# One product with the state for new values and outputs, outputs kept by token rows, and moved loads, in a DeltaNet and attention encoder layer

## What is computed

```python
proj = rms_norm(h) @ w_in                # q, k, v of the delta rule, z, a, b, attention q, k, v, two gates
# delta rule, both directions, 8 value heads on 4 key heads, chunks of 64 tokens
v_new = u_i - w_i @ state
o     = qd_i @ state + aqk_i @ v_new
state = state * exp(gl_i) + kd_i.T @ v_new
o_dn  = rms_norm(o_fwd + o_bwd, dn_out_norm) * silu(z)      # norm over the 128 numbers of a head
y_dn, y_at = o_dn @ w_dn_branch, attention(q, k, v) @ w_attn_branch
h = h + (sigmoid(gate_dn) * y_dn + sigmoid(gate_at) * y_at) @ w_o
h = h + square(relu(rms_norm(h) @ w_up)) @ w_down           # then a gated per-layer embedding
```

## Time and profile before

| What | us |
|---|---|
| median of 3 runs (lowest to highest) | 3044.26 (3043.36 to 3045.45) |
| profiled execution | 3044.7 |
| its span in the trace | 3042.9 |
| PE busy in the span | 2870.0 (94%) |
| DVE, ACT, POOL busy | 1537.4, 915.6, 318.0 |

### The profile page before, as it was taken

The page is one execution under the profiler, slowest core; times in us unless marked ns, Lnnn a source line. Parts: engine busy times, 40 slices in busy tenths (PEclk is TensorE's granted clock), DMA queues, the critical chain, the costliest instruction groups (busy, mean ns, idle before and its releaser), DMA issues. The chain is left out here.

```text
span 3042.9 us, 40696 instructions
## 1 busy us (share of the span) xinstructions
PE 2870.0 (94%) x17223; PEld 2430.7 (80%) x17223; DVE 1537.4 (51%) x2164; ACT 915.6 (30%) x1238; POOL 318.0 (10%) x418
## 2 busy tenths in 40 slices
PE   6999989997996999799999999999999999999999
PEld 5878878886785999688886788888888888888787
DVE  4556638995782443477753423333433433433732
ACT  4674432123440222244434502321111112112321
POOL 0000110000004666100002100100000000000200
PEclk8999999998997999899999999999999999999999
DMA  6227874226347565311125541111111111110121
GB/s 196 64 88 181 233 226 128 78 82 190 119 128 199 169 183 147 125 36 36 35 76 195 205 145 61 35 42 35 40 37 35 42 35 35 42 35 28 57 63 50
DMA packets 304516, 299.65 MB, mean 98 GB/s; under 512 B 53494, under 2 KB 258880, under 8 KB 303568
## 3 DMA queue, kind: packets, MB, share of 16 engines
q1 hardware_dynamic: 297840, 261.47, 28.9%
q0 software_dynamic: 6496, 35.59, 3.5%
HBM read 205.67 MB, written 84.79 MB: 95 GB/s over the span
## 5 line engine op out<-in xcount | busy, mean ns | idle before, releaser
L176 ACT ACTIVATE w_hi<-w_stage 128x1024 fp32r<-128x1024 f32 x149 | 157.2, 1056 | 930.4 <-PE psum L1637 928.7
L1637 PE MATMUL psum<-x_hi,w_hi 128*128 128x512 f32 (+1 forms) x1536 | 386.3, 360 | 7.6 <-issue 4.7
L1637 PE MATMUL psum<-x_lo,w_hi 128*128 128x512 f32 (+1 forms) x1536 | 383.7, 358 | 0.0
L1637 PE MATMUL psum<-x_hi,w_lo 128*128 128x512 f32 (+1 forms) x1536 | 383.2, 358 | 0.0
L701 PE MATMUL psum<-u_hi,w_hi 128*128 128x512 f32 (+1 forms) x1272 | 344.7, 380 | 7.5 <-PEq L218 7.5
L1920 DVE TENSOR_TENSOR tail_h<-tail_h,psum 128x1280 f32<-128x1280 f32 x136 | 202.1, 1486 | 248.9 <-PE psum L1637 248.9
L701 PE MATMUL psum<-u_lo,w_hi 128*128 128x512 f32 (+1 forms) x1272 | 321.1, 361 | 0.0
L701 PE MATMUL psum<-u_hi,w_lo 128*128 128x512 f32 (+1 forms) x1272 | 319.8, 360 | 0.0
L1637 PEld LDWEIGHTS psum<-x_hi,w_hi 128*128 128x128 f32 x1536 | 256.2, 188 | 53.9 <-issue 7.8
L1637 PEld LDWEIGHTS psum<-x_lo,w_hi 128*128 128x128 f32 x1536 | 255.6, 188 | 45.5
L1637 PEld LDWEIGHTS psum<-x_hi,w_lo 128*128 128x128 f32 x1536 | 255.5, 188 | 45.5
(11 more groups left out here) (217 smaller groups left out, 3943.6 us busy)
## 6 DMA issues: line engine op xcount, KB each, us to landing
w_stage<-in_w_in_dram SPq DMA_DIRECT2D x53, 512.0 KB, 4.9
w_stage<-in_w_up_dram SPq DMA_DIRECT2D x32, 512.0 KB, 4.2
w_stage<-in_w_down_dram SPq DMA_DIRECT2D x32, 512.0 KB, 3.7
dc_rows<-rows_gc_beta SPq DMA_DIRECT2D x40, 256.0 KB, 6.2
gates<-pj_out SPq DMA_DIRECT2D x16, 640.0 KB, 2.9
st_v<-dn_v SPq DMA_DIRECT2D x20, 512.0 KB, 6.3
st_decay<-rows_decay SPq DMA_DIRECT2D x20, 512.0 KB, 6.7
dn_o<-st_ob SPq DMA_DIRECT2D x80, 128.0 KB, 2.0
```

The costliest lines, as they stand in the source:

```text
L176: e.activation(self.hi[:, J % 2, :] if out is None else out, src, ACT.Copy).then_inc(self.high_done, 1)
L1637: ins = e.matmul(acc_chunk(core, t % 2, c), wt[:, k, cols], x(k)[:, n0:n1], start=(k == 0 and n == 0), stop=(k == n_k - 1 and n == 2))
```

## The change

Five parts.

1. The order of the projection tiles: the ropes stand at 20, 22, 24, 36, 38 and so on to 48, each with a plain tile behind it, and a plain slot of the solves has room for 13600 instead of 13000 modelled nanoseconds, a rope slot 5800 instead of 5200.
2. The first iteration's inputs of the delta phase are loaded inside `phase_proj`, on SP at its last weight-load step, ahead of the store of the last tile, into a set of buffers `first`, which lies over buffers of the ropes. The four inverse loads wait for POOL's stores of the inverses (`u_stored`). The attention's first queries, keys and values are loaded by SP inside `phase_delta`, behind the third iteration's inputs.
3. In a unit, the `w` rows and the scaled queries lie in one ring (`nq`, half of `w`, `qd`, other half of `w`), so that one 128-column stationary block times the state gives new values in one half of the partitions and outputs in the other. `from_state` is gone. The product of `aqk` is turned round (`aqk` 64 x 64 stationary, new values moving), so outputs come by token rows. PE's order in a turn of the loop is new_values(n, 0), new_values(n-1, 1), w_rows(n+1), from_values(n, 0), from_values(n-1, 1). Copies that took 128 partitions in one go take 64 in two.
4. `dn_o` is laid out by tokens ([2, TOK, VH*P]); a unit stores four DMAs of 64 rows of 1 KB instead of two of 256 rows of 512 B. The tail loads a head as 1280 rows of 512 B for each direction.
5. The head norm in the tail goes by token rows: DVE sums squares over a row (`tensor_reduce`), ACT takes a small square root, DVE a reciprocal and a broadcast multiply, PE turns the head back with ten transposes inside the next column tile (`turn_head`), and DVE applies gain and z straight from PSUM (`gate_head`). The three ones matmuls, the Ln, the Exp and their table loads, and the two DVE multiplies go. POOL no longer waits for its store to land before it loads the next head.

The core of the diff:

```diff
 def proj_tiles():
-    order += [("z", 0), ("rope", 0), ("rope", 1), ("rope", 2)]
-    late_rope = (38, 39, 40, 41, 44, 46, 48)
+    ropes_at = (20, 22, 24, 36, 38, 40, 42, 44, 46, 48)
...
 def solve_shares():
-            room += 5200 if ... == "rope" else 13000
+            room += 5800 if ... == "rope" else 13600
...
 # phase_proj, SP
+                    if t == N_IN - 1:
+                        heads_are_stored(e)
+                        load_state_inputs(e, 0, first, state_src, S.first_landed)
+                        e.wait_ge(S.first_zeroed, 1)
+                        e.wait_ge(S.u_stored, 32 + 32 * SPLIT)
+                        load_state_inverses(e, 0, first[5], d_u, S.first_landed)
...
+                e.wait_ge(S.first_landed, 16 * 14)
...
 # phase_delta, SP
+                for h in range(2):
+                    e.dma_start(q_in[:, h].bitcast(F32), d_q[h].rearrange("n p t -> p n t")).then_inc(S.at_landed, 16)
+                e.dma_start(k_in[:, :, :].bitcast(F32), d_keys[0].rearrange("n p t -> p n t")).then_inc(S.at_landed, 16)
+                e.dma_start(v_in[:, :, :], d_values[:, :, 0:P]).then_inc(S.at_landed, 16)
...
-                        e.dma_start(dst[d, 2 * g:2 * g + 2, :, i * P:(i + 1) * P].rearrange("h p t -> p h t"),
-                                    ob[:, n % OUTS, 2 * d:2 * d + 2, :]).then_inc(stored[n % OUTS], 16)
+                        for h in range(2):
+                            tok = tile_at(it, d) * P + CH * h
+                            e.dma_start(dst[d, tok:tok + CH, 2 * g * P:(2 * g + 2) * P], ob[half(1 - h), n % OUTS, own(d), :].rearrange("p h v -> p (h v)")).then_inc(stored[n % OUTS], 16)
...
 # phase_delta, PE
                 def new_values(n, step):
-                    if n >= 1:
-                        e.wait_ge(vnew_ready[step], n)
+                    if n >= 2 - step:
+                        e.wait_ge(o_out[step], n - 1 + step)
...
+                    for c in range(4):
+                        h = half_at(step, c // 2)
+                        e.matmul(out[:, c, :], nq[:, n % RING, c, P * h:P * h + P], state[:, g, c, :], start=(c == 0), stop=False, skip_group_check=True)
                     for c in (0, 2, 1, 3):
-                        e.matmul(ps_vn[step][h, hd, :], u_b[:, it % DEPTH, d, 2 * g + hd, h], vb[:, n % RING, c, :], start=True, stop=False)
-                        ins = e.matmul(ps_vn[step][h, hd, :], nw[:, n % RING, c, h], state[:, g, c, :], start=False, stop=True)
+                        ins = e.matmul(out[h, c, :], u_b[it % DEPTH][:, d, 2 * g + hd, h], vb[:, n % RING, c, :], start=False, stop=False, skip_group_check=True)
-                def from_state(n, step):
-                    for c in range(4):
-                        e.matmul(ps_o[step][d][:, hd, :], state[:, g, c, :], qd[:, n % RING, c, half(half_at(step, d))],
...
                 def from_values(n, step):
-                            e.matmul(ps_o[step][d][:, hd, :], vnew[h, step, hd, :], aqk[h, it % DEPTH, d, 2 * g + hd, :], ...)
+                            e.matmul(ps_no(n, step)[half(1 - h), 2 * d + hd, :], aqk[it % DEPTH][half(h), d, 2 * g + hd, :], vnew[half(h), step, hd, :], ...)
...
 # phase_delta, ACT
                 def output(n, step):
-                    e.wait_ge(updated[step], n + 1)
+                    e.wait_ge(s_full[step], n + 1)
                     if step == 0 and n >= OUTS:
-                        e.wait_ge(stored[n % OUTS], 32 * (n // OUTS))
+                        e.wait_ge(stored[n % OUTS], 64 * (n // OUTS))
...
 # phase_tail, POOL
-                    for buf, src in ((a, d_on[0]), (b, d_on[1]), (z, d_z)):
-                        e.dma_start(buf[:, j % 2, :], src[j]).then_inc(o_landed[j % 2], 16)
+                    for buf, src in ((a, d_on[0]), (b, d_on[1])):
+                        e.dma_start(tokens(buf[:, j % 2, :]), src[:, j * P:(j + 1) * P].rearrange("(t p) c -> p t c", p=P)).then_inc(o_landed[j % 2], 16)
+                    e.dma_start(z[:, j % 2, :], d_z[j]).then_inc(o_landed[j % 2], 16)
                 def store_gated(j):
-                    e.wait_ge(S.gated, j + 1)
-                    e.dma_start(d_og[j], a[:, j % 2, :]).then_inc(S.o_stored, 16)
-                    e.wait_ge(S.o_stored, 16 * j + 16)
+                    head_is_gated(e, j)
+                    e.dma_start(d_og[j], sq[:, j % 2, :]).then_inc(S.o_stored, 16)
...
 # phase_tail, PE, inside the column tile, after k = 1, 2, 3 (the last tile: 0 to 2 and 4 to 6)
+                def turn_head(j, c):
+                    e.wait_ge(S.normed, j + 1)
+                    aux_is_free(e, 3 * j + c)
+                    for i in range(n0, n1, P):
+                        ins = e.transpose(aux(3 * j + c)[:, i - n0:i - n0 + P], a[:, j % 2, i:i + P], ct["ident"])
+                    ins.then_inc(S.aux_full, 1)
...
 # phase_tail, DVE
+                norm_head(0)
                 for j in range(KT - 1):
                     take_attn(j)
                     weight(tile_attn(j) + 2)
-                    norm_head(j)
+                    if j < KT - 2:
+                        norm_head(j + 1)
+                        gate_head(j)
+                    else:
+                        gate_head(j)
+                        norm_head(j + 1)
```

More of the change, by code:

```diff
@@ L403, in solve_shares @@
         while done < len(costs):
-            room += 5200 if slot < N_IN + 2 and TILES_IN[slot - 2][0] == "rope" else 13000
+            room += 5800 if slot < N_IN + 2 and TILES_IN[slot - 2][0] == "rope" else 13600
             first = done
@@ L448, in acc_is_taken, with heads_are_stored @@
         e.wait_ge(acc_free[t % 2], t // 2 + 1)
+    def heads_are_stored(e):
+        for p in range(2):
+            e.wait_ge(rope_stored[p], 32 * (len(ropes) // 2))
     def aux_is_full(e, u):
@@ L457, in phase_proj @@
         big = lambda name: sb(nc, c2, "pj_" + name, [P, TOK])
+        with ExitStack() as c3:
+            first = state_inputs(nc, c3, "first")
         y, sq, r = big("y"), big("sq"), big("r")
-        s, tk, out = ([big(f"{n}{i}") for i in range(2)] for n in ("s", "tk", "out"))
+        s, tk = ([big(f"{n}{i}") for i in range(2)] for n in ("s", "tk"))
         cos, sin = big("cos"), big("sin")
+        out = [big(f"out{i}") for i in range(2)]
         ab_T = tk[1]
@@ L1164, in take_values @@
                         e.wait_ge(s_full[step], n)
-                    e.tensor_copy(vnew[:, step], ps_vn[step]).then_inc(vnew_ready[step], 1)
+                    for d in range(2):
+                        h = half(half_at(step, d))
+                        ins = e.tensor_copy(vnew[h, step], ps_no(n, step)[h, own(d), :])
+                    ins.then_inc(vnew_ready[step], 1)
                 def update(n, step):
@@ L1336, in values @@
                             e.wait_ge(S.second_out, seconds(n) + 1)
[L1337 removed]
+                        ins = e.matmul(out_at(n), v[h // GROUP][:, first + j, :], pT[:, n % 2, j * P:(j + 1) * P], start=(j == 0), stop=(j == count - 1))
                     ins.then_inc(S.o_full, 1)
@@ L1517, in slot_used, with head_is_gated @@
             acc_is_full(e, last_tile_of(before))
+    def head_is_gated(e, j):
+        for u in range(3 * j, 3 * j + 3):
+            e.wait_ge(aux_free[u % 2], u // 2 + 1)
     def aux_is_free(e, u):
@@ L1639, in accumulate @@
                             ins.then_inc(S.x_used, 1)
-                        if between is not None and k == n_k // 2 - 1:
-                            between()
+                        if between is not None and k in between:
+                            turn_head(*between[k])
                     ins.then_inc(S.acc_full, 1)
```

257 lines of the change are left out of this document (131 added, 126 removed).

## The result

The changed kernel takes 3025.13 us (median of 5 runs, 3022.71 to 3032.36); the kernel before took 3043.36 in the same runs. The ratio is 0.9943, 95% interval 0.9928 to 0.9958: faster by 18 us, clear of the noise, where 51 was forecast and 24 was the least of the range. The profiled execution took 3027.76 us, its span is 3026.0. Two executions further down, one of the kernel with late loads (14237 us) and one of the combined kernel (3487), took far longer than the others of the same kernel, and the medians leave them out.

A forecast was written before the change was run, and what follows sets the result against it. Projection and attention branch had PE waits to remove; the delta units were PE-bound. Terms −46 −12 +4 +3 +3 −9 +6 = −51 took 3044.7 to 2994 us, range 2948 to 3020.

The forecast's parts named there:

- Projection order: Projection: reordered tiles remove the stalls behind ropes, less a new wait for DVE; −46 us, bounds −51 and −38.
- The 50.8 us of the ropes: Projection: time lost in tiles 22, 23 and 40 to 42, which follow ropes in a row; all 50.8 us should go.
- PE waits about 5 us: Projection, ahead of rope 36: larger solve shares cost DVE 7 us against a lead of 2.1, so PE waits about 5.
- rival b: DVE bounds the projection, its lag growing in the rope pairs and solves ending behind the last tile; 3009 us, chance 0.1.
- First inputs: Start of the delta phase: inputs loaded early bring the first new value sooner; −12 us, bounds −17 and −5.
- The unit: Delta phase: fewer products but 13 paid shape changes make a unit 7.39 us; +4 us over 40, bounds −35 and +24.
- rival a: Delta phase: shape changes inside from_values cost nothing, unit 6.41 us, store waits +14 instead of +3; 2966 us, chance 0.2.
- Stores: Delta phase: ACT's waits for output stores reach PE, +3 us (0 to 9); attention loads ahead of first stores, +3 (0 to 8).
- Attention's first loads: Start of attention: loading its first inputs early removes 9 of the 14.05 us before its first score; −9, bounds −6 and −9.
- Tail: Attention branch at the end: PE gains, but a cycle of waits sets the pace; +6 us, bounds −13 and +15.
- The ring: Tail: cycle of store, loads, add, norm and gate across POOL, ACT, DVE and PE; 20.2 us a head against 18.0.
- Rival c: Tail: short rows land late and eat the gain; +20 gives 3008 us, landing near 15.5 gives 3045 or more; chance 0.13.

The follow-up runs named there:

- the kernel with late loads: Changed kernel with the attention's four loads issued after unit 31 instead of ahead of the first output stores; median 3019.08 us, ratio 0.9917.
- the combined kernel: Changed kernel with old solve rooms, from_values regrouped, attention's loads after unit 31, six output buffers and gate_head before norm_head; medians 2947.83 and 2946.26 us.
- both regroupings: Changed kernel with from_values' aqk products before its kd products, 3020.4 us; the five-edit kernel with products sorted by shape across two steps, 2920.46 us.
- e7: Changed kernel with from_values regrouped, the attention's loads after unit 31 and six output buffers instead of three; median 2988.44 us, ratio 0.9818.
- e9: Kernel with all five edits, plus a unit's products sorted by stationary shape across its two steps; median 2920.46 us, ratio 0.9595.

## Why the prediction was wrong

The sign was right, and each mechanism that it named took place. But most terms were too kind, two mechanisms were missed (the slower clock behind a wait, and POOL's loads against SP's), and the measured 3025 lies 5 us above the range.

1. *Projection order, −46, measured −35.8.* The 50.8 us of the ropes did go; 15.0 came back, where the sum had 5. The step that failed is "PE waits about 5 us" as the whole of what comes back. That wait was right: 5.1 us ahead of tiles 35 to 37, for DVE's low parts, as forecast. But the sum took it as idle time alone. Behind it PE worked at half the granted clock for 5.4 us, and the stall cost 8.3 (the old rooms take exactly that away). The rows showed this price: of the 34.1 us lost in tiles 40 to 42, 24.7 are idle time (82.62 − 57.96) and 9.4 longer PE work, at a granted clock of 0.86. And the stall at tile 45, 6.7 us (5.2 idle, 1.5 longer work), stood nowhere in the sum: POOL's 4 MB, which held up no swap in the kernel before, met the swaps and the weight tile's load here. The bytes could be seen: the stretch of tiles 40 to 42 shows 187 GB/s, nearly three times the 67 of a plain tile. Of rival b only the one wait came; the rope pairs broke even, as was held against it.
2. *First inputs, −12, measured −8.9.* The solves ended 1.5 us ahead of the last matmul (889.3 against 890.83), not 6.4 as I had it. It was luck that only 3 of these 4.9 us were lost: from there to the first new value the sum had 27.0, and it took 24.9. The mechanism and the bounds held.
3. *The unit, +4, measured +12 (40 × 0.30).* That all 13 changes are paid, 64 x 64 against 64 x 128 among them, was right; rival a is refuted by the steps of 0.37 and 0.42 and by both regroupings, and the sentence of the Trainium skill that I cited (TensorEngine Tiling (Array Packing), Tiling Modes, Key Properties) agrees with the trace: a change of shape costs 0.17 us. The mis-sized term is the short group: I took 0.37 for all eight, and the four that end in `kd` take 0.42, four times 0.05, which is the 0.2 between 7.39 and 7.59. Two slips change nothing: the prices as written give 7.41, and the 6.41 of rival a doesn't follow from them (without the eight changes they give 6.2).
4. *Stores, +3 and +3, measured about +7.* The units beyond 40 × 7.59 hold 12.7 us, against 5.7 beyond 40 × 7.29 before. The sum was nearly right and its split wrong: the one unit that meets the attention's loads takes 9.1 of it (16.7 instead of 7.59), and its slower clock was not in the term. The later input batches cost nothing in the changed kernel and some 6 us with the late loads (313.1 against 307); with units of 6.9 they cost 15.4 us of waits (26.6 without that unit's 11.2), about the +14 of rival a.
5. *Attention's first loads, −9, measured −8.3.* Right.
6. *Tail, +6, measured +16.2.* The ring was named rightly, with the engines in it; a head's way round it was 21.2 us (127.0 for tiles 2 to 7), not 20.2: 0.7 more of landing and 0.5 more from the add to the store, 0.2 less for the issues. That is 6 us over six heads. The rest is the ends of the stage: six heads at 20.2 instead of 18.0 are +13, so the +6 let the first two heads and the last two tiles take back 7, and they took back 2.4. The working of that 7 is nowhere shown, so which part of it failed stays open; what the trace shows there is tile 1, where PE is idle for 6.8 us (POOL waited 9.3 for the first head's loads) and its granted clock is 0.86. Rival c is refuted: the landing was 7.7 us, far from 15, and the gate-first run shows that the same landing costs tiles 2 to 6 nothing once the ring is cut. The issue of a load of 1280 rows took 1.94 / 2 = 0.97 us, against 0.53 for 128; I had 1.1.

The range was too narrow at its upper end because I gave each term its own bounds and then the sum less than their sum: projection −38, inputs −5, unit +24, stores +17, attention −6 and tail +15 together reach +7, past the time before. All the errors lay on that side. Two have one reason: behind a removed wait I asked only what is late next, not what else had been going on beside it, nor at what clock PE works behind a wait.

Not settled: the changed kernel's runs spread over 9.7 us and those of most edits over 4 to 13, the kernel before over 3 to 5. With six output buffers they spread over 2.3 (e7) and 1.9 (e9), but over 7.6 and 8.2 in the combined kernel, so the store waits alone do not explain it.

## What to carry to other kernels

Before a stall is struck from a sum, look at what else ran inside it: its DMA share and its busiest other engine are candidates for the next bound, and a big transfer that cost nothing there can hold up the next weight load. Price a wait of PE with the slower stretch behind it, where the rows show one: compare PE's busy time with that of an undisturbed tile. Where PE is the bound and works with small stationary blocks, count the changes of shape as well as the products, and sort the list by shape across independent steps: here that was worth more (7.59 to 6.23 us a unit) than the product that the change saved. Where one engine's list mixes the end of one item with the start of the next, put first what frees a buffer; a load that is issued behind such a step turns the whole way round into the pace.

## What was unexpected on the hardware side

Four swap DMAs of 160 KB on SP took 14.99 us to issue while eight transfers of 512 KB from POOL were under way, and 6.39 with a quarter of those bytes: here the issuing queue itself is held, and with it every load behind. It is not so each time: in the kernel before the same eight transfers were under way and the four took 2.42. After a wait of 4.37 us PE worked at half the granted clock for 5.4 us, so that a stall with 5.1 us of idle time cost 8.3. A group of two 64 x 128 matmuls takes 0.05 us more than one of two 64 x 64 matmuls with the same moving columns (0.42 against 0.37). All groups of a unit fit one pattern: over their passes of 0.055 or 0.11 us, those with 64-column blocks (`u_b` 0.58, `aqk` 0.37) pay 0.14 to 0.15, those with 128-column blocks (`nq` and `w_rows` 1.09, `kd` 0.42) 0.20.
